# A projection's first two chunks in halves of 128 tokens, ahead of and behind the transposes of the second tile

## What is computed

```python
def odd_mixer(h, w_in, dw_w, dw_b, ln_g, ln_b, conv_w, conv_b, A_log, dt_bias, D_skip, norm_w, w_out):
    b, S, _ = h.shape
    proj = h @ w_in
    glu_a = proj[..., :CONV_CH]
    glu_b = proj[..., CONV_CH:2 * CONV_CH]
    ...
    g = glu_a * jax.nn.sigmoid(glu_b)
    g = depthwise_conv(g, dw_w, dw_b, CONV_K // 2, CONV_K // 2)
    ...
# in second_block
    x = x + 0.5 * rms_norm(swiglu(rms_norm(x, nw[0]), ffn_w_gate[l, 0], ffn_w_up[l, 0], ffn_w_down[l, 0]), nw[1])
    hn = rms_norm(x, nw[2])
    ...
    x = x + rms_norm(m, nw[3])
```

## Time and profile before

| | us |
|---|---|
| median of three runs | 3019.81 |
| lowest and highest | 3017.77, 3023.1 |
| the profiled execution | 3015.07 |
| its span | 3013.3 |

### The profile page before, as it was taken

How to read it: one execution, slowest core, us unless ns; L and a number is a source line. 1 busy time by engine, 2 the same in 40 slices (tenths; PEclk the granted TensorE clock), 3 DMA queues, 4 the chain that set the end, 5 groups by cost and what they waited for, 6 DMA issues and landing times.

```text
span 3013.3 us, 36188 instructions
## 1 busy us (share of the span) xinstructions
PE 2837.4 (94%) x14132; PEld 2347.6 (78%) x14132; DVE 1985.1 (66%) x2581; ACT 1450.6 (48%) x2123; POOL 170.0 (6%) x162
## 2 busy tenths in 40 slices
PE   5999989889999999999898999998999999979999
PEld 4877878757888888888796788787788787966787
DVE  7778775777788797865536555555754555697654
ACT  4454453475454454544536544444644444444543
POOL 0000000000000000000130000000000000592000
PEclk9999999999999999999999999999999999889999
DMA  8667664206677687975541455555255554430553
GB/s 320 207 242 267 231 224 154 91 1 237 224 261 252 211 294 260 306 212 185 215 139 56 154 182 196 182 185 198 98 188 192 188 187 173 151 112 1 180 188 128
DMA packets 100552, 562.74 MB, mean 187 GB/s; under 512 B 20256, under 2 KB 20768, under 8 KB 43936
## 3 DMA queue, kind: packets, MB, share of 16 engines
q1 hardware_dynamic: 100384, 560.43, 53.3%
HBM read 559.30 MB, written 1.09 MB: 186 GB/s over the span
## 4 chain that ended last, share of the span: by engine, by line
PE 79%; DVE 9%; ACT 5%; DMA 3%; issue 3%; SPq 0%; DVEq 0%; ACTq 0%
PE banks L359 24%; PE banks L361 24%; PE banks L360 23%; PE banks L835 2%; DVE w_rest L346 2%; ACT w_high L336 1%; DVE od_xbc L2009 1%; DVE od_glu L1968 1%; DMA ada_tiles<-in_w_ada 1%; DMA post_mod<-post_scale 1%; PE banks L2313 1%; DVE ada_terms L432 1%; PE banks L658 1%; PE banks L2282 1%; DVE post_term L539 1%
## 5 line engine op out<-in xcount | busy, mean ns | idle before, releaser
L346 DVE TENSOR_TENSOR w_rest<-w_raw,w_high 128x2048 fp32r<-128x2048 f32 x426 | 978.9, 2299 | 539.8 <-ACT w_high L336 539.4
L336 ACT ACTIVATE w_high<-w_raw 128x2048 fp32r<-128x2048 f32 x426 | 810.8, 1907 | 239.9 <-PE banks L361 200.7
L359 PE MATMUL banks<-w_high,u_parts 128*128 128x512 f32 (+1 forms) x2160 | 828.7, 384 | 32.9 <-DVE post_term L539 15.3
L361 PE MATMUL banks<-w_high,u_parts 128*128 128x512 f32 (+1 forms) x2160 | 817.1, 378 | 0.0
L360 PE MATMUL banks<-w_rest,u_parts 128*128 128x512 f32 (+1 forms) x2160 | 816.0, 378 | 0.0
L359 PEld LDWEIGHTS banks<-w_high,u_parts 128*128 128x128 f32 x2160 | 410.6, 190 | 106.5 <-issue 22.6
L361 PEld LDWEIGHTS banks<-w_high,u_parts 128*128 128x128 f32 x2160 | 410.1, 190 | 76.4
L360 PEld LDWEIGHTS banks<-w_rest,u_parts 128*128 128x128 f32 x2160 | 410.8, 190 | 71.0
L359 PE MATMUL banks<-w_high,gated_high 128*128 128x512 f32 x968 | 379.2, 392 | 4.8 <-DVE w_rest L346 3.6
L361 PE MATMUL banks<-w_high,gated_rest 128*128 128x512 f32 x968 | 376.9, 389 | 0.0
L360 PE MATMUL banks<-w_rest,gated_high 128*128 128x512 f32 x968 | 376.8, 389 | 0.0
(11 more groups left out here) (259 smaller groups left out, 2807.6 us busy)
## 6 DMA issues: line engine op xcount, KB each, us to landing
w_raw<-in_w_ffn_in SPq DMA_DIRECT2D x242, 1024.0 KB, 4.9
w_raw<-in_w_ffn_out SPq DMA_DIRECT2D x121, 1024.0 KB, 4.9
ada_tiles<-in_w_ada SPq DMA_DIRECT2D x128, 512.0 KB, 5.3
w_raw<-in_w_mix SPq DMA_DIRECT2D x54, 1024.0 KB, 4.9
w_raw<-in_w_mix_out SPq DMA_DIRECT2D x22, 1024.0 KB, 4.9
ada_first<-in_w_ada SPq DMA_DIRECT2D x7, 1024.0 KB, 16.7
post_gain_row<-post_mod SPq DMA_DIRECT2D x10, 512.0 KB, 6.3
na_bias<-in_na_bias SPq DMA_DIRECT2D x1, 4096.0 KB, 14.1
```

What stands on the lines that cost most here:

```text
L336: act.activation(w_high(g)[:, 0:n], raw[:, g % RING, 0:n], ACT.Copy).then_inc(w_hi_ready, 1)
L346: nc.vector.tensor_tensor(w_rest(g)[:, 0:n], raw[:, g % RING, 0:n], w_high(g)[:, 0:n].bitcast(F32), ALU.subtract).then_inc(w_lo_ready, 1)
L359: nc.tensor.matmul(ps, hi_a, hi_b, start=first_, stop=False)
L361: return nc.tensor.matmul(ps, lo_a, hi_b, start=False, stop=last_)
```

## The change

For sublayer 10 the transposes of tile 1 leave the hand-over. A new function does a part of a chunk for 128 tokens, 24 matmuls of 128 columns for each column tile. Before the transposes of tile 1 stand chunk 0 (both column tiles) and tile 0 of chunk 1 for the first 128 tokens; behind them tile 1 of chunk 1 for the first 128 tokens, then chunks 0 and 1 for the second 128. Chunks 2 to 16 are as before, and so are all other engines.

```diff
         def hand_over_pe(s):
 
             turn_pe(s, 0, 0)
-            if s == 10:
-                turn_pe(s, 0, 1)
...
+            def pe_tokens(self, c, tiles, tt):
+
+                pe = nc.tensor
+                g = self.g0 + c
+                tok = slice(tt * P, (tt + 1) * P)
+                await_rest(pe, g)
+                await_u(pe, self.s, 0, tt)
+                for m in tiles:
+                    e = 2 * c + m
+                    if e >= 2 and tt == 0:
+                        pe.wait_ge(y_taken, 4 * PASSES.index((self.s - 1, 0)) + 4)
+                    for k in range(KT):
+                        cols = slice(k * CHUNK + m * P, k * CHUNK + (m + 1) * P)
+                        ins = three(bank[e][:, tok], w_high(g)[:, cols], u[:, 0, 0, k, tok], w_rest(g)[:, cols],
+                                    u[:, 0, 1, k, tok], k == 0, k == KT - 1)
+                if tt == 1 and tiles[-1] == 1:
+                    ins.then_inc(w_used, 1)
...
             def pe(self, pe):
                 S = self.sem
-                for c in range(17):
+                self.proj.pe_tokens(0, (0, 1), 0)
+                self.proj.pe_tokens(1, (0,), 0)
+                turn_pe(10, 0, 1)
+                self.proj.pe_tokens(1, (1,), 0)
+                self.proj.pe_tokens(0, (0, 1), 1)
+                self.proj.pe_tokens(1, (0, 1), 1)
+                for c in range(2, 17):
                     self.proj.pe_chunk(c)
```

## The result

The changed kernel took 3022.68 us in the median of twelve runs (3017.07 to 3041.06), the kernel before 3018.86 in twelve of its own (3014.19 to 3023.10). The medians differ by 3.8 us, 0.13%. The ratio is 1.0027, with a 95% interval of 1.0014 to 1.0040; it follows the means, which differ by 8.5 us, because a few slow executions lift the mean more than the median. So the changed kernel is slower by 0.27%, just past the 0.2% that the prediction called measurable. The times are not one bunch: seven of the twelve lie between 3017 and 3023, five between 3031 and 3041. The profiled execution is one of the five, 3031.56 us with a span of 3029.8.

What follows compares the result with a forecast made beforehand. PE was taken as the bound, idle 10.39 and 1.50 us at the hand-over to sublayer 10. Gone: 1.5 us wait, 0.8 us slow transposes, 14.07 us matmuls; added: 13.4; 3.0 us, or 2 against the 3019.81 median: 3018, range 3014 to 3039.

Steps and rivals of the forecast that it cites:

- Clock kept, the forecast: 0.38: PE's clock stays at full rate through the new 1.6 us gap at the hand-over to sublayer 10; 3018 us, chance 0.38.
- The 3.0 us at chunk 2: At full clock and 112 ns per matmul, chunk 2 starts at 2580.6 against 2583.59, 3.0 us sooner.
- The three courses: PE's clock in the new gap: kept (3018), fallen and brought back by transposes (3024), or fallen and staying down (3037).
- rival 1: Clock falls in the new gap and the second tile's transposes bring it back; 3024 us, chance 0.31.
- rival 2: Clock falls in the new gap and stays down through the narrow matmuls; 3037 us, chance 0.21.
- The 2 us that a kept clock should win: Whole kernel: gain against the median of 3019.81 if the clock stays up, giving 3018.
- A 128-column matmul: In chunks 0 and 1, each was priced at 112 ns at 2.4 GHz and 213 ns at 1.2 GHz.
- Rival 3: Narrow operands stream at a quarter rate, 227 ns per 128-column matmul in chunks 0 and 1; 3038 us, chance 0.07.
- rival 4: The skill's 81 ns per 128-column matmul holds in chunks 0 and 1; 3013 us or a little less, chance 0.03.
- The new place of the wait: Tile 0 of chunk 1 waits for bank 2, freed at 2561.67 while chunk 0 runs until 2562.7; cost nothing.
- Or brings it back: Rival 1's support: from 2704.18 sixteen slow transposes and two matmuls ran back to back; at 2708.30 the clock was up.
- That the gain passes whole to the end: From chunk 2 on, later PE, ACT and DVE work moves along, so the profiled 3015.07 us would be 3012.1.

Runs made afterwards that it cites:

- e2: Changed kernel with 7 unused 512-column matmuls in the gap before the new work and 2 before the second turn; 3017.88 us, ratio 0.9995.
- e4: Against the kernel before: both turns first as before, then chunks 0 and 1 as 192 matmuls of 128 columns; 3047.09 us, ratio 1.0096.
- e8: The changed kernel unaltered, one more single traced run; 3021.50 us.
- e3: Changed kernel with tile 0 of chunk 1 ahead of chunk 0 in the front part, which lengthens the gap; 3040.72 us, ratio 1.0078.
- e9: Smaller dose of the change: only chunk 0 in halves around the second turn, chunk 1 whole in 256 columns; 3024.22 us, ratio 1.0019 against the kernel before.
- e7: The changed kernel unaltered, second sitting of eleven runs; median 3020.75 us, ratio 1.0009, traced execution 3018.77 us.
- e1: Kernel before with 43 unused 512-column matmuls between the two turns of sublayer 10 and 6 behind the second; 3014.27 us, ratio 0.9990.
- e10: The changed kernel unaltered, third sitting of twelve runs; median 3020.60 us, ratio 1.0018.

## Why the prediction was wrong

The time, 3022.68, lies in the range. But the forecast was 2 us faster than before, and the changed kernel is slower: by 3.8 us in the medians, by the ratio of 1.0027 over all runs.

**The step that failed** is "Clock kept, the forecast: 0.38". The 3.0 us at chunk 2 need the clock to stay at 1.00 through the new gap. It fell in three of the four traces of the changed kernel, each time 1.0 to 1.1 us into the new work; chunk 2 came 15.3, 15.4 and 4.2 us later than before, and 3.0 us sooner only in the fourth. The three courses were named and had a price each, and I took the one with the largest chance as the forecast. But a median over runs that fall into courses of -2, +4 and +18 us is not the likeliest course: by my own chances 0.41 lay at the forecast or below it and 0.59 above, so the median was rival 1's 3024; it is 3022.68. That the middle executions took rival 1's course is not shown: their times can't tell it, since with the clock held (e2) runs reach 3021.88. The chance of slower (0.30) was too low for the same reason: a few runs of rival 2 lift the mean of the ratio past 0.2%.

**The prices held.** From the first transpose to chunk 2, forecast and measured: clock kept 26.0 and 25.9; rival 1 32.5 and 33.1; rival 2 44.7 and 44.3. The times of the traced executions: 3018 forecast and 3018.77 seen, 3024 and 3021.50, 3037 and 3031.56 and 3035.22, with 3041.06 at the top. The 2 us that a kept clock should win against before are in no median: with the clock held (e2), the changed kernel's is 3017.88 against 3017.61, though the interval of that ratio (0.9986 to 1.0004) leaves room for them.

**A 128-column matmul**: 112 ns taken at 2.4 GHz, 112.0 measured; 213 ns at 1.2 GHz, and e4's 192 took 41.0 us, 213.5 ns each. Rival 3 (227) and rival 4 are out. The Trainium skill, TensorE: Matmul & The Clock Gate, section "Back-to-back issue gap", has 81 ns for such a pair of weight load and matmul; for these 4-byte operands the trace disagrees by 31 ns.

**The new place of the wait** for the product with the post gain cost nothing where the clock stayed: the 72 matmuls run through without a gap.

**"Or brings it back"**: sixteen slow transposes were offered as evidence that eight at the second turn could do so. In one of the three traces in which the clock had fallen (e8) it came back 1.6 us behind them; in the other two it did not, nor in e3, e4 and e9, whose second turn ran at the low clock too. That is one in six, so rival 1's 0.31 against rival 2's 0.21 was not borne out by the traces, though six are few. Times above 3029, rival 2's, were 5 of 12, 0 of 11 and 3 of 12 in the three sittings.

**That the gain passes whole to the end** held within some 2 us: the two distances moved together in every trace (-3.2 and -3.3 with the filler before, +15.3 and +17.6 in the changed kernel, +25.1 and +27.3 with the halves behind, -11.4 and -11.5 at 256 columns). Chunk 2 beginning slow cost 1.8 us in the changed kernel, as summed (1.5 to 2.5). But e7 won 3.0 us at chunk 2 and only 0.7 at the end. There the clock, which falls in chunk 4 with its 32 columns in most traces (6.83 us in the kernel before), was down for longer, and chunk 4 took 7.7 us instead of 6.5:

```profile
2599.16:2609.41 10.25, 10.25 (x50) 10.25 (x50) 8.25 (x8) 2.08 (x3) 10.00 (x8) 0.50 0.37 136
```

That is 1.2 of the 2.3 us; at the hand-over to sublayer 11 1.8 us of the gain are left. The other 1.1 are lost at the second turn of that hand-over, behind a gap of 2.01 us in both traces. These are its transposes and the clock over them, in the kernel before and then in e7 (columns as in rows 3 and rows 6):

```profile
2828.24 1.32 PE L658 MATMUL banks<-identity,normed 128*128 128x128 f32 x8 [2.01 <-DVE normed L625]
2828.23:2831.64 3.41, 3.28 (x17) 2.50 (x18) 1.97 (x3) 2.61 (x5) 0.00 (x0) 1.00 0.00 0
```
```profile
2830.84 1.78 PE L658 MATMUL banks<-identity,normed 128*128 128x128 f32 x8 [2.01 <-DVE normed L625]
2831.27:2834.68 3.41, 3.41 (x13) 2.58 (x11) 1.56 (x3) 2.59 (x5) 0.00 (x0) 0.50 0.00 0
```

From the first transposes of that hand-over to the end are 196.8 us in the traces in which the clock stayed there (before, e1, e2, e3, e8) and 197.9 to 198.0 in those in which it fell (the changed kernel's first, e10, e4, e7, e9). The prediction took no account of this second place; it accounts for 1.1 of the 17.6 us in the changed kernel as well.

**What stays open**: what decides, behind one and the same gap of 1.67 us, whether the clock falls; and why none of eleven runs went above 3027 in one sitting when five of twelve went above 3031 in another. If it were chance from execution to execution alone, with 8 in 35, none in eleven would come once in some 17 sittings. The second and third sittings were on different chips, so chip and sitting can't be told apart here.

## What to carry to other kernels

Work moved into a gap pays at the clock that it meets there, so price a move at both clocks, and look in the trace for the same stream at the low one: does it ever end the stretch? Cutting the moving operand from 256 to 128 columns doubled the number of matmuls, at 112 ns each where 256 columns take 120, and a fallen clock came back under them in one trace only, right behind a turn, and in e4 not for 41.00 us; swapping which operand is stationary kept 256 columns, moved more work into the same gap, and won 0.29%. Where a course differs from run to run, forecast the median of the mixture, not its likeliest member.

## What the runs showed of the hardware

For float32r, 32 and 128 columns cost the same 112 ns at 2.4 GHz (e7), and 32, 128 and 256 columns the same 213 ns at 1.2 GHz (chunk 4 of e7, e4). I had not expected how stubborn the low clock is: 41.00 us of uninterrupted 128-column matmuls left it at 0.50, while the same stream held 1.00 for 8.2 and 14.5 us in e7. The Trainium skill, TensorE: Matmul & The Clock Gate, section "Why this matters for your kernels", advises to keep TensorE continuously busy to reach the full clock; by the row of e4 being busy was not enough.
